# Hybrid mixer and conv-GLU layer on one core: inputs laid out by the host, and both RMS norms applied to the products instead of to the rows

## The reference

```
h   = rmsnorm(x, norm1_w)                       # x * rsqrt(mean(x*x) + 1e-6) * w
p   = h @ w_in                                  # q k v | z | xbc | dt | qk_m | v_m | o_m | i f
att = moba_attention(rms(q), rms(k), v)         # 8 heads of 64; causal in one block of 256
ssm = mamba2_ssd(z, xbc, dt, ...)               # conv(4)+silu, 2 chunks of 128, gated norm
ml  = mlstm_chunkwise(qk_m, v_m, o_m, i, f, ..) # conv(4)+silu, 4 heads of 128, gated norm
x2  = x + concat(att, ssm, ml) @ w_out          # 2048 -> 1024
g, v = split(rmsnorm(x2, norm2_w) @ ffn_w_up)   # 2 x 2816
out = x2 + (gelu(conv3(g)) * v) @ ffn_w_down    # 2816 -> 1024
```

## Time and profile before

| what | us |
|---|---|
| median of 3 runs | 441.48 |
| profiled execution, its span from first to last instruction | 440.2 |
| what lies around the span, by the median (no other time of the profiled execution is recorded) | 1.3 |
| TensorE busy | 420.8 |
| VectorE busy | 278.1 |
| ScalarE busy | 247.3 |
| GpSimd busy | 31.9 |
| DMA, mean over the span | 161 GB/s |

### The profile page before, as it was taken

The page is one execution under the profiler, slowest core; times in us unless marked ns, Lnnn a source line. Parts: engine busy times, 40 slices in busy tenths (PEclk is TensorE's granted clock), DMA queues, the critical chain, the costliest instruction groups (busy, mean ns, idle before and its releaser), DMA issues.

```text
span 440.2 us, 6837 instructions
## 1 busy us (share of the span) xinstructions
PE 420.8 (96%) x2716; PEld 378.8 (86%) x2716; DVE 278.1 (63%) x384; ACT 247.3 (56%) x325; POOL 31.9 (7%) x24
## 2 busy tenths in 40 slices
PE   3799999999999999989999699999999999999996
PEld 3699999878888888767888699999999999999995
DVE  2769849947564688778744755655655655656553
ACT  6568887583466764988434545544544544444430
POOL 2004426401010000000000000000000000000000
PEclk9999999999999999999999699999999999999999
DMA  7775455653534323325546085656655655566202
GB/s 200 237 251 165 132 184 190 194 191 113 174 98 149 136 98 104 127 103 204 170 153 192 0 269 163 208 160 191 188 177 181 190 186 191 191 191 191 95 1 95
DMA packets 45485, 70.80 MB, mean 161 GB/s; under 512 B 4926, under 2 KB 27670, under 8 KB 45462
## 3 DMA queue, kind: packets, MB, share of 16 engines
q1 hardware_dynamic: 45462, 70.48, 49.4%
HBM read 69.42 MB, written 1.05 MB: 160 GB/s over the span
## 4 chain that ended last, share of the span: by engine, by line
PE 91%; ACT 4%; DVE 2%; DMA 2%; issue 1%; SPq 0%; DVEq 0%
PE pj L1088 23%; PE pj L1090 23%; PE pj L1089 23%; PE mx L1134 6%; PE mx L1088 4%; PE mx L1089 4%; PE mx L1090 4%; PE mx L1131 2%; DMA wraw<-in_w_in 2%; ACT whi L383 1%; ACT L519 1%; DVE wlo L705 1%; ACT sz_b L519 0%; DVE acc L1043 0%; ACT seg_b L526 0%
## 5 line engine op out<-in xcount | busy, mean ns | idle before, releaser
L705 DVE TENSOR_TENSOR wlo<-wraw,whi 128x2048 fp32r<-128x2048 f32 x60 | 137.4, 2291 | 106.0 <-ACT whi L383 105.9
L383 ACT CAST whi<-wraw 128x2048 fp32r<-128x2048 f32 x65 | 123.9, 1908 | 110.4 <-PE pj L1090 80.1
L1088 PE MATMUL pj<-hT_hi,whi 128*128 128x256 f32 x512 | 147.1, 287 | 3.3 <-DVE hT_lo L724 3.3
L1089 PE MATMUL pj<-hT_lo,whi 128*128 128x256 f32 x512 | 146.5, 286 | 0.0
L1090 PE MATMUL pj<-hT_hi,wlo 128*128 128x256 f32 x512 | 146.5, 286 | 0.0
L1088 PEld LDWEIGHTS pj<-hT_hi,whi 128*128 128x128 f32 x512 | 100.1, 195 | 4.5 <-DVE wlo L705 3.4
L1089 PEld LDWEIGHTS pj<-hT_lo,whi 128*128 128x128 f32 x512 | 100.1, 196 | 0.3
L1090 PEld LDWEIGHTS pj<-hT_hi,wlo 128*128 128x128 f32 x512 | 99.9, 195 | 0.0
L1088 PE MATMUL pj<-whi,hT_hi 128*128 128x512 f32 x144 | 57.7, 401 | 0.0
L1090 PE MATMUL pj<-whi,hT_lo 128*128 128x512 f32 x144 | 56.2, 390 | 0.0
L1089 PE MATMUL pj<-wlo,hT_hi 128*128 128x512 f32 x144 | 56.1, 390 | 0.0
(11 more groups left out here) (202 smaller groups left out, 440.8 us busy)
## 6 DMA issues: line engine op xcount, KB each, us to landing
wraw<-in_w_in SPq DMA_DIRECT2D x24, 1024.0 KB, 5.2
wraw<-in_ffn_w_up SPq DMA_DIRECT2D x44, 512.0 KB, 4.7
wraw<-in_ffn_w_down SPq DMA_DIRECT2D x11, 1024.0 KB, 4.8
wraw<-in_w_out SPq DMA_DIRECT2D x8, 1024.0 KB, 4.8
x_sb<-in_x SPq DMA_DIRECT2D x2, 512.0 KB, 4.0
out_x<-x_sb SPq DMA_DIRECT2D x1, 512.0 KB, 2.7
out_x<-x_sb SPq DMA_DIRECT2D x2, 256.0 KB, 2.0
seg_b<-in_w_in SPq DMA_DIRECT2D x1, 64.0 KB
```

Of the source, the lines that this page charges most:

```text
L383: nc.scalar.copy(whi[:, slot, :], wraw[:, slot, :]).then_inc(s.hi_done, 1)
L705: nc.vector.tensor_tensor(wlo[:, slot, :], wraw[:, slot, :], whi[:, slot, :].bitcast(F32), ALU.subtract).then_inc(s.lo_done, 1)
L1088: pe_mm(ps, a_hi, b_hi, start=start, stop=False, skip_group_check=shared)
L1089: pe_mm(ps, a_hi, b_lo, start=False, stop=False, skip_group_check=shared)
```

## The change

The host now lays the inputs out: xT (x transposed), each weight unit as one row of 8 KB in each partition, the small projection as one array, and all parameters as one array `par` of 128 x 238. Then:
- The kernel loads xT and `par` by ScalarE's DMA queue, and units 0 and 1 in four pieces each by SP's. ScalarE and VectorE take the eight channel blocks one at a time, each with its piece of the weights. TensorE waits piece by piece. The raw x goes into hT; it isn't normed.
- GpSimd squares xT and adds the squares up in three steps; TensorE sums them over the partitions with a matrix of ones (`x_norm`, behind unit 1, where the small projection now stands too). VectorE and ScalarE make 1/rms of it, as a row over all partitions (`rb`, 128 x 260) and as columns.
- Everything that reads products of w_in multiplies by 1/rms: the soft-plus rows, a new step `conv_scale` for the conv groups (its result `cg` in SBUF is what base and taps read), and the evacuations of v, z and o by a scale, now in two halves each. The norms of q and k take the scale into their epsilon.
- The second norm likewise: the rows of x2 are turned as they are, its 1/rms is made meanwhile, and the gate and the value are multiplied by it in each step (`gate_scale`). TensorE writes the second half of x2 in two parts. The row of 1/rms is made by TensorE behind the first two up units (`x2_norm`).

The diff, cut to its core:

```diff
@@ SP queue
+            for u in range(2):
+                for k in range(4):
+                    sp.dma_start(wraw[:, u, piece(k)], A["w_in"][u, :, piece(k)]).then_inc(first_pieces[u][k], 16)
+            sp.dma_start(wraw[:, 2, :], A["w_in"][2, :, :]).then_inc(wdma[2], 16)
+            sp.dma_start(w24, A["w_small"].rearrange("p (k n) -> p k n", k=KD)).then_inc(s.small_in, 16)
...
-                sp.dma_start(d[:, :, 0:256], up_unit(j, half, 0)).then_inc(wdma[slot], 16)
-                sp.dma_start(d[:, :, 256:512], up_unit(j, half, FH)).then_inc(wdma[slot], 16)
+                sp.dma_start(wraw[:, slot, :], A["w_up"][bass.ds(j * (2 * P) + half * P, P), :]).then_inc(wdma[slot], 16)
@@ GpSimd
+            def squares(piece_, n):
+                half = slice(piece_ * 1024, (piece_ + 1) * 1024)
+                v = xn[:, piece_, :]
+                pool.tensor_tensor(sq[:, half], v, v, ALU.mult).then_inc(s.sq_done, 1)
+                pool.wait_ge(s.sq_done, n)
...
+            for i, w in enumerate((1024, 512, 256)):
+                pool.tensor_tensor(sq[:, 0:w], sq[:, 0:w], sq[:, w:2 * w], ALU.add).then_inc(s.sq_done, 1)
@@ ScalarE
-                group_computed(g)
+                act.wait_ge(s.cg_ready, 2 * g + b + 1)
...
-                    nc.scalar.activation(acc[:, b, i, :], pj[g % 2][:, k * T:(k + 1) * T], ACT.Identity,
+                    nc.scalar.activation(acc[:, b, i, :], cg[:, b, i, :], ACT.Identity,
...
-            at(0, rows_softplus)
+            at(1, rb_root)
+            at(1, rows_softplus)
...
+            act.dma_start(par[:, :], A["par"][:, :]).then_inc(s.par_in, 16)
+            for i in range(4):
+                act.dma_start(xT[:, 2 * i:2 * i + 2, :], A["xT"][:, 2 * i:2 * i + 2, :]).then_inc(xt[i], 16)
+            act.wait_ge(s.par_in, 16)
+            for c in range(KD):
+                x_hi(c)
+                split_piece(c // 4, c % 4)
...
-            row_norm([(s.x2_ready, 1), (s.x2_ready, 2)], s.ssq2, s.ms2, s.rt2, 4, U_FFN + 1)
+            x2_square(0)
+            split(U_FFN + 1)
             transposed_hi(s.h2_ps, s.h2_hi, hT_hi, p_n2, 4)
+            x2_square(1)
+            x2_root()
@@ VectorE
+            def x_lo(c):
+                dve.wait_ge(s.hi_T, c + 1)
+                nc.vector.scalar_tensor_tensor(out=hT_lo[:, c, :], in0=xT[:, c, :], scalar=par[:, p_n1 + c:p_n1 + c + 1],
+                                               in1=hT_hi[:, c, :].bitcast(F32), op0=ALU.mult, op1=ALU.subtract).then_inc(s.lo_T, 1)
...
+            def rb_scale():
+                dve.wait_ge(s.ssq_ps, 1)
+                link(nc.vector.tensor_scalar(rms_e[:, :], bank[1][:, T:T + 2 * NT], EPS / D, EPS * EPS, ALU.mult, ALU.add))
+                nc.vector.tensor_scalar(rb[:, :], bank[1][:, 0:T + 2 * NT], 1.0 / D, EPS, ALU.mult, ALU.add).then_inc(s.rb_ms, 1)
+                dve.wait_ge(s.rb_rt, 1)
+                nc.vector.reciprocal(rb[:, :], rb[:, :]).then_inc(s.rb_ready, 1)
...
+            def conv_scale(g, b):
+                dve.wait_ge(s.unit_done, 2 * g + 2)
...
+                nc.vector.tensor_tensor(cg[:, b, :, :], pj[g % 2][:, b * 512:(b + 1) * 512].rearrange("p (i t) -> p i t", i=2),
+                                        rbc(2), ALU.mult).then_inc(s.cg_ready, 1)
...
-                        ins = nc.vector.scalar_tensor_tensor(out=acc[:, b, i, back:T], in0=pj[g % 2][:, k * T:(k + 1) * T - back],
+                        ins = nc.vector.scalar_tensor_tensor(out=acc[:, b, i, back:T], in0=cg[:, b, i, 0:T - back],
...
             split(U_FFN + 1)
+            transposed_lo(s.h2_hi, s.h2_lo, hT_hi, hT_lo, p_n2, 4, 2)
...
+            dve.wait_ge(s.rb2_ps, 1)
+            nc.vector.tensor_copy(rb[:, 0:T], bank[0][:, 0:T]).then_inc(s.rb2_ready, 1)
+            dve.wait_ge(s.rb2_ready, 1)
...
             for c in range(2):
                 split(step_unit(0, c))
@@ TensorE
-            at(0, params_turn)
-            at(0, small_proj)
+            at(1, small_proj)
+            at(1, x_norm)
...
-            turn_rows(s.x2_rows, s.h2_ps)
+            pe.wait_ge(s.x2_ready, 1)
+            turn_x2(0, range(KD))
...
             for half in range(2):
                 up_half(0, (U_FFN + half) % NR, U_FFN + half, half, s.h2_lo)
+            x2_norm()
```

More of the change, by code:

```diff
@@ L211, in landed @@
         def landed(u):
[L213 to L218, removed]
+            return 16 * (u // NR + 1)
         def step_landed(i, c):
-            return i * (16 if c == 2 else 32) + landed(U_FFN + 2 + c)
+            return i * 16 + landed(U_FFN + 2 + c)
         def up_count(i):
@@ L383, in split, with x_hi, split_piece, rb_root @@
                 nc.scalar.copy(whi[:, slot, :], wraw[:, slot, :]).then_inc(s.hi_done, 1)
[L385 to L395 removed]
+            def x_hi(c):
+                act.wait_ge(xt[c // 2], 16)
+                nc.scalar.activation(hT_hi[:, c, :], xT[:, c, :], ACT.Copy, scale=par[:, p_n1 + c:p_n1 + c + 1]).then_inc(s.hi_T, 1)
+            def split_piece(u, k):
+                act.wait_ge(first_pieces[u][k], 16)
+                nc.scalar.copy(whi[:, u, piece(k)], wraw[:, u, piece(k)]).then_inc(s.hi_done if k == 3 else s.hi_piece, 1)
+            def rb_root():
+                act.wait_ge(s.rb_ms, 1)
+                nc.scalar.activation(rb[:, :], rb[:, :], ACT.Sqrt).then_inc(s.rb_rt, 1)
+            def x2_square(t):
+                act.wait_ge(s.x2_ready, 2 * t + 1)
+                if t:
+                    act.wait_ge(s.ssq2, t)
+                nc.scalar.activation(junk, x_sb[:, t, :], ACT.Square, accum_out=stat[:, 4 + t:5 + t]).then_inc(s.ssq2, 1)
+            def x2_root():
+                act.wait_ge(s.ms2, 1)
+                nc.scalar.activation(stat[:, 6:8], stat[:, 6:8], ACT.Sqrt).then_inc(s.rt2, 1)
             def transposed_hi(ps_sem, hi_sem, dst, pcol, banks):
@@ L476, in mv_copy @@
                 group_computed(G_MV)
-                nc.scalar.copy(vaug[:, :, :, 0:P],
-                               pj[G_MV % 2][:, :].rearrange("p (c h d) -> p c h d", c=NT, h=MH)).then_inc(s.mv_ready, 1)
+                for c in range(NT):
+                    nc.scalar.activation(vaug[:, c, :, 0:P], pj[G_MV % 2][:, c * 512:(c + 1) * 512].rearrange("p (h d) -> p h d", h=MH),
+                                         ACT.Copy, scale=rcol(c)).then_inc(s.mv_ready, 1)
             def cst_copy():
@@ L1008, in _ @@
             at(27, transposed_lo, s.ssmT_hi, s.ssmT_lo, hT_hi, hT_lo, p_sn, 4)
[L1010 to L1014 removed]
+            dve.wait_ge(s.par_in, 16)
+            for c in range(KD):
+                x_lo(c)
+                split_piece(c // 4, c % 4)
             dve.wait_ge(s.w24_hi, 1)
```

421 lines of the change are left out of this document (224 added, 197 removed).

## The result

| | before | after |
|---|---|---|
| median | 441.88 us (441.07 to 443.26, 4 runs) | 466.3 us (464.64 to 469.19, 4 runs) |
| ratio, 95% interval | | 1.0555 [1.051, 1.0601]: slower |
| span of the profiled execution | 440.2 | 463.1 (its own time 464.88) |

The account below looks back on a forecast made before the run. TensorE bounds the kernel (91% of the chain). Span 440.2 +20.9 (state products) +0.3 (z) -1.95 (second norm) +0.7 (tail) +3.6 (clock) = 463.7, +1.3 = 465.0 us; range 440.5 to 468, likeliest case 455 to 468.

Parts of the forecast that it names:

- The likeliest case: Whole kernel: GpSimd and VectorE exclude each other in head and taps; 465.0 us; chance together with Case (d) 0.47.
- rival (a): Whole kernel: GpSimd does not hold VectorE up; order alone puts state products at 89.6; 446.2 us; chance 0.27.
- (b): As rival (a), chain some 2 to 3 shorter, no low clock in one or both places; about 441.3 us; chance 0.13.
- The exclusion: Head and conv taps: GpSimd's instructions hold up VectorE's with two SBUF inputs for their whole length; +20.9 us at state products.
- Case (d): VectorE keeps its turn in the head, is held only in the taps; +13, about 457; counted in the forecast's 0.47.
- First matmul: Head: first big matmul at 6.3 instead of 14.47, a gain of 8.2 us; bounds 5.5 and 7.5.
- GpSimd's head work: Head: two squares and three sums, 8.7 us, come between VectorE's 16 instructions; last chunk ready at about 22.3.
- Chain after the sums: Before soft-plus: 1/rms chain with a reciprocal of 1.7 to 1.8 us; soft-plus starts at 34.5 with exclusion, +8.1.
- Groups 0 to 2: Conv groups: taps wait for GpSimd's splits until 46.3, 63.5 and 81.3; +10.1, +13.8 and +18.6 us.
- State products: After the conv groups: TensorE takes them up at 108.5 instead of 87.6, +20.9 us with exclusion.
- Clock: Low clock after TensorE's idles before the state products and behind the second norm: +1.8 us each, bounds 0 and 3.5.
- Rival (c): Order does not bind, TensorE keeps most of the 8.2 gained in the head, no clock lost; 432.9 us; chance 0.13.

Follow-up runs that it names:

- run 1: Changed kernel, but conv taps read the raw products in PSUM instead of cg in SBUF, the scaling left out of the taps: 453.0 us, ratio 1.0269.
- run 12: Separate kernel computing nothing of the layer: GpSimd's SBUF work beside VectorE instructions of nine kinds; GpSimd's subtraction took 4.51 us unhindered, 6.41 behind a long VectorE instruction.
- run 2: Changed kernel, but ScalarE makes the squares of xT and VectorE adds them after the chunks, instead of GpSimd: 461.31 us, ratio 1.0466.
- run 3: Changed kernel with taps from PSUM (scaling left out of them) and squares and sums off GpSimd together: 447.95 us, ratio 1.0153.
- run 9: Kernel before with only the change's second norm put in; first norm, loads and GpSimd's work as before: 442.21 us, ratio 1.0004.
- run 10: Kernel before with the change's second norm, VectorE splitting units 34 and 35 before it waits for the turned 1/rms row: 437.69 us, ratio 0.9903.
- run 4: Changed kernel, but VectorE splits units 34 and 35 before it waits for the turned 1/rms row: 460.69 us, ratio 1.0471.
- run 7: Changed kernel with the edits of run 2 and run 4, and conv products scaled in place in PSUM, where bases and taps read them: 443.49 us, ratio 1.0045.
- run 11: Kernel before with only the weight loads from the host's tiles; norms, x and parameters as before: 441.49 us, ratio 0.9994.

## Why the prediction was right

The likeliest case came about, by its own mechanism. The time alone would not show that: the outer range, 440.5 to 468, holds rival (a) and part of (b) as well. What decides are the signs, the held taps and the places of the waits. The terms one by one:

- **The exclusion** was inferred from two thin rows: GpSimd stretched by 0.33 of the 0.44 us that VectorE had left, and by 0.05 of 0.19; the second is no whole remainder. It is shown in the other direction by the held taps, by run 1, and directly by run 12. Case (d), exclusion in the taps only, fell: the head's subtractions are held too (2.12, 2.11, 2.84).
- **First matmul**: 6.3 was predicted, 9.73 measured, outside my bounds. The x piece landed at 6.55, not 4.2, and ScalarE's function table load (1.28) stands behind that wait, where I had no term for it:

```profile
6.55 1.28 ACT L371 ACT_TABLE_LOAD   x1 [6.55 <-DMA xn<-in_xT]
7.84 0.51 ACT L371 ACTIVATE hT_hi<-xn,par 128x256 fp32r<-128x256 f32 x1
```

- **GpSimd's head work**: 8.7 by half and quarter of the 2048 columns' rate from the earlier trace rows. It took 2.01+1.98+4.99 = 9.0, but with a gap, and it held VectorE's 16 up by 7.2, not 8.7. So the last chunk was ready at 23.8, 1.5 later than predicted and not 3.4, and TensorE needed 3.3 behind it where the forecast had 5.0. Unit 1 ended at 27.16 (predicted 27.3) and the sums were there at 30.78 (30.8). The late start and these two errors cancelled; that the sum came out is luck.
- **Chain after the sums**: 1.78 for the reciprocal over 260 columns (1.7 to 1.8), soft-plus at 34.16 (34.5). The slope from the rows of 1 and 16 columns was right, and the estimate of 2.2 was 0.4 too high (the repeat count that it rests on stands in the Trainium skill, VectorE: DVE Perf Modes, "First, the fixed hardware budget", not in the section that the prediction names).
- **Groups 0 to 2**: held until 45.8, 62.8, 80.5, as in the forecast (46.3, 63.5, 81.3). The tap held at 105.39, in group 4, was not in it, where GpSimd was to be through before the taps: it cost half a microsecond.
- **State products**: +20.9 predicted, +19.5 measured. z: +0.6 (+0.3). Idle before unit 34: 2.85 (2.95). Second norm with its clock: -0.1 (-0.15). Tail: +0.8 (+0.7).
- **Clock**: 1.8 twice was predicted; I read 2.1 at the state products and 1.7 behind the second norm. That it falls behind an idle of 2.8 is a chance and not a rule: with the same 2.84 at the second norm the profiles of runs 2 and 3 have the low clock, those of runs 1 and 9 do not.
- **Rival (a)**, 446.2, comes near run 3 (447.95). **Rival (b)** needed a reciprocal of 0.4 and matmuls from 5.5; they were 1.78 and 9.73. **Rival (c)** could not be: with both exclusions gone the state products still come 4.5 later than before.

The net by part, from the runs: taps against GpSimd's splits 13.3, squares against the chunks 5.0, VectorE's order at the second norm 4.5 (runs 9 and 10) to 5.6 (run 4). Added up, these are 23 to 24 of the 24.4 lost (466.3 - 441.9), by the ratios 20 to 21; run 7, which has all three repairs at once, gives 22.8 (22.5). What is left, run 7 against the kernel before, is +1.4 (medians) to +2.0 (ratio). I put it down to the first norm's new chain ahead of the soft-plus rows, whose state products still start 4.2 late in run 7 (91.82), less the 4 us that the second norm brings in run 10. The first norm's part was not run alone.

The host's layout of the weights was worth nothing by itself (run 11). That of x was not run alone; its effect here was that the norm had to be applied later.

## What to carry to other kernels

Before a copy is put between PSUM and its reader, look which engines read SBUF beside it: the same product left in PSUM was 13 us faster here than in SBUF. A VectorE instruction whose maximum is many times its median, and that ends with a GpSimd instruction, was here a stall that the busy share counts as work. When a change mixes several ideas and loses, put each into the kernel before by itself: one of three here was worth 1%, after two lines changed places.

## What the runs showed of the hardware that I had not expected

All but the last are from run 12, one execution.

- A multiplication of a single SBUF tile by a constant is shut out by GpSimd's subtraction (4.58 us instead of 0.28); a reciprocal, also one tile, is not (1.695, four times).
- GpSimd and VectorE take turns: GpSimd waited for one VectorE instruction (6.41 instead of 4.51), then went ahead of the next, which was queued right behind it (6.58 instead of 2.29).
- The reciprocal costs 6.6 ns a column at 256 columns (1.695 us), four times an addition of the same width (0.41).
- A select of GpSimd on SBUF shuts VectorE out as its subtraction does (2.22), its memset does not (0.42).
- The same idle of TensorE at the second norm, 2.84 us, was followed by the low clock (0.50, 1.2 GHz) in three profiles (the changed kernel, runs 2 and 3) and not in two (runs 1 and 9).
